# Modulation sums spread over the input tiles, and mLSTM norms set between the output tiles, in an fp32 two-block kernel

## The reference

```python
mod = silu(c) @ w_ada + b_ada                       # 6 x 1024 values: sh1, sc1, gt1, sh2, sc2, gt2
h = rmsnorm(x, g_norm1) * (1 + sc1) + sh1
z = h @ w_in                                        # glu_a, glu_b, q, k, v, o, i, f, g_a, g_b
u = causal_dwconv(glu_a * sigmoid(glu_b))           # 31 taps
y_a = silu(layernorm(u)) @ w_conv_out
q, k = silu(causal_dwconv(q, k))                    # 4 taps
hm = mlstm(q, k, v, i, f)                           # 4 heads of 128: weighted scores, numerator,
                                                    # denominator max(|den|, exp(-m)), division
hm = layernorm_per_head(hm) * m_norm_g * sigmoid(o)
y_b = hm @ w_m_out
x = x + gt1 * ((sigmoid(g_a) * y_a + sigmoid(g_b) * y_b) @ w_out)
...                                                 # then router, experts, and a second block
```

## Time and profile before

| | us |
|---|---|
| median of 3 runs | 2563.48 (2561.7 to 2565.02) |
| the profiled execution | 2564.16 |
| its span, first to last instruction | 2562.4 |
| PE busy in the span | 2313.2 |
| DVE busy in the span | 1182.8 |
| ACT busy in the span | 813.5 |
| mean granted TensorE clock | 0.942 of full speed |

### The profile page before, as it was taken

The page is one execution under the profiler, slowest core; times in us unless marked ns, Lnnn a source line. Parts: engine busy times, 40 slices in busy tenths (PEclk is TensorE's granted clock), DMA queues, the critical chain, the costliest instruction groups (busy, mean ns, idle before and its releaser), DMA issues.

```text
span 2562.4 us, 29704 instructions
## 1 busy us (share of the span) xinstructions
PE 2313.2 (90%) x11748; PEld 1584.8 (62%) x11748; DVE 1182.8 (46%) x1716; ACT 813.5 (32%) x1251; POOL 119.6 (5%) x160
## 2 busy tenths in 40 slices
PE   6899878959999999957989498999999899999997
PEld 3688636623333333324768496888777787888775
DVE  3789345430000000025654743677843573677832
ACT  3222333321111111124455253323324283323322
POOL 0000000021111111100000200000000000000000
PEclk8999978979999999978989689999999999999999
DMA  8622200628999999830111001122222301222221
GB/s 356 226 79 92 92 0 33 277 91 332 375 378 399 386 389 385 359 137 34 66 66 66 1 34 66 66 98 98 99 99 99 132 1 66 81 90 95 95 99 66
DMA packets 36406, 384.56 MB, mean 150 GB/s; under 512 B 10080, under 2 KB 10336, under 8 KB 13408
## 3 DMA queue, kind: packets, MB, share of 16 engines
q1 hardware_dynamic: 27520, 374.91, 37.5%
q0 software_dynamic: 8800, 8.45, 1.0%
HBM read 384.10 MB, written 16.83 MB: 156 GB/s over the span
## 4 chain that ended last, share of the span: by engine, by line
PE 53%; DVE 16%; ACT 5%; issue 3%; DMA 1%; DVEq 1%; POOL 0%; ACTq 0%; SPq 0%; POOLq 0%
PE PS L744 9%; PE PS L570 9%; PE PS L571 9%; PE PS L572 8%; PE PS L783 4%; PE PS L764 4%; DVE ring_r L1946 3%; PE PS L791 2%; DVE A L1694 2%; ACT w_hi_r L1318 2%; PE PS L533 2%; DVE A L2156 1%; DVE sq L2154 1%; DVE A L2157 1%; DVE hid_r L2169 1%
## 5 line engine op out<-in xcount | busy, mean ns | idle before, releaser
L571 PE MATMUL PS<-h_r,w_hi_r 128*128 128x512 f32 x1104 | 432.5, 392 | 0.0
L570 PE MATMUL PS<-h_hi_r,w_hi_r 128*128 128x512 f32 x1056 | 418.0, 396 | 10.8 <-ACT A L1345 7.5
L572 PE MATMUL PS<-h_hi_r,ring_r 128*128 128x512 f32 x1056 | 413.3, 391 | 0.0
L1946 DVE TENSOR_TENSOR ring_r<-ring,w_hi_r 128x1024 fp32r<-128x1024 f32 x196 | 238.6, 1223 | 362.7 <-ACT w_hi_r L1318 362.7
L1318 ACT ACTIVATE w_hi_r<-ring 128x1024 fp32r<-128x1024 f32 x196 | 202.6, 1051 | 329.0 <-PE PS L572 203.9
L570 PEld LDWEIGHTS PS<-h_hi_r,w_hi_r 128*128 128x128 f32 x1056 | 199.7, 189 | 62.3 <-issue 17.2
L571 PEld LDWEIGHTS PS<-h_r,w_hi_r 128*128 128x128 f32 x1104 | 209.2, 190 | 45.0 <-issue 1.9
L572 PEld LDWEIGHTS PS<-h_hi_r,ring_r 128*128 128x128 f32 x1056 | 199.6, 189 | 42.1
L1922 DVE TENSOR_TENSOR A<-A,PS 128x512 f32<-128x512 f32 x16 | 11.0, 687 | 396.4 <-PE PS L744 396.4
L744 PE MATMUL PS<-A 128*64 128x512 f32 x768 | 170.4, 600 | 0.1
L570 PE MATMUL PS<-x_r,top_r 128*128 128x512 f32 x320 | 128.2, 400 | 12.0 <-DVE ring_r L1605 12.0
(11 more groups left out here) (448 smaller groups left out, 3762.6 us busy)
## 6 DMA issues: line engine op xcount, KB each, us to landing
A<-wexp SPq DMA_DIRECT2D x64, 2048.0 KB, 12.3
ring<-wall SPq DMA_DIRECT2D x63, 2048.0 KB, 8.1
ring<-wexp SPq DMA_DIRECT2D x16, 2048.0 KB, 18.1
h<-wexp SPq DMA_DIRECT2D x16, 2048.0 KB, 13.2
A<-wada SPq DMA_DIRECT2D x12, 2048.0 KB, 14.7
x<-xt_in SPq DMA_DIRECT2D x2, 2048.0 KB, 12.1
A<-y_assignments SPq DMA_DIRECT2D x4, 1024.0 KB, 7.9
h_tokens<-A SPq DMA_DIRECT2D x4, 512.0 KB, 2.8
```

The source lines that it names most:

```text
L570: mm(out, w[0], x_[0], start=first, stop=False)
L571: mm(out, w[0], x_[1], start=False, stop=False)
L572: return mm(out, w[1], x_[0], start=False, stop=last_)
L1946: tt(ring_r[:, slot, :, cols], ring[:, slot, :, cols], w_hi_r[:, :, cols].bitcast(F32), ALU.subtract).then_inc(S("w_lo"), 1)
```

## The change

1. SP: unit 0 is issued before quarter 4. Quarters 6 and 7 are now DVE's as well; quarters 8, 9 are issued before unit 3, 10 and 11 before unit 5, each when its buffer is free.
2. PE, prologue: each `ada_cols` follows its own `ada_rows`; rows of quarter 4 come after the gate products. ACT's copy of them moves behind the x_r copies.
3. PE, input tiles: rows only of quarter 5; columns of quarters 4 to 11 one at a time after tiles 0, 1, 8, 9, 16, 17, 20 and 21, in three banks, with four `mod_ev`.
4. The transposes of v come after tile 36, the conv mean and gate columns after tile 37, the conv variance after tile 38; ACT's copies, SiLUs and squares move with them. Heads' convolutions go in the order q0, k0, q1, k1, ...
5. Heads: numerators alternate between banks 6 and 3; DVE weights head h + 1 before it divides head h; the row of exp(-m) comes after the next scores; the conv norm's scaling and SiLUs sit behind head 0's weights.
6. Out tiles: tiles wait for their own bank (`mix_bank`) instead of a whole group; means of the heads stand before tile 2, variances before tile 4; the DVE norm operations are interleaved with the gating.

```diff
-                if a in (4, 5):
-                    sp.wait_ge(S("ada_row"), a - 3)
-                elif a in (6, 7, 8, 9):
-                    sp.wait_ge(S("ada_row"), a - 1)
-                elif a >= 10:
-                    sp.wait_ge(S("ada_used"), a - 9)
+                if 4 <= a < 8:
+                    sp.wait_ge(S("ada_row"), a - 3 if a < 6 else a - 1)
+                elif a >= 8:
+                    sp.wait_ge(S("ada_used"), a - 7)
...
+            load_first(0)
             load_ada(4)
-            load_first(0)
...
-            for a in range(6, 10):
+            for a in range(6, 8):
                 load_ada(a)
             for u in range(2, NU1):
-                if u == 3:
-                    for a in range(10, 12):
+                if u in (3, 5):
+                    for a in range(u + 5, u + 7):
                         load_ada(a)
...
-            ada_rows(0)
-            for a in range(1, 4):
+            for a in range(4):
                 ada_rows(a)
-                ada_cols(a - 1, 1)
-            ada_cols(3, 1)
-            ada_rows(4)
+                ada_cols(a, 1)
...
+            ada_rows(4)
...
-                    if g == 0:
-                        ada_cols(4 + j, 6)
-                        if j < 3:
-                            ada_rows(5 + j)
...
+                    if j < 2 and g in (0, 2, 4, 5):
+                        n = (0, 2, 4, 5).index(g)
+                        ada_cols(4 + 2 * n + j, MOD_BANK[n])
+                    if p == 0:
+                        ada_rows(5)
+                    if p == 36:
+                        v_rows()
+                    if p == 37:
+                        conv_mean()
+                        gate_columns()
+                    if p == 38:
+                        conv_var()
...
             for hd in range(MH):
                 if hd:
-                    pe.wait_ge(S("ml_h"), hd)
-                head_row(hd, 5, gr[7])
+                    pe.wait_ge(S("ml_ad"), hd)
                 for s in range(NT):
                     pe.wait_ge(S("ml_p"), NT * hd + s + 1)
-                    mm(PS[:, 6, s * P:T], A[:, 16 + s, hd * P:(hd + 1) * P], A[:, 52 + s, s * P:T], start=s == 0,
+                    mm(PS[:, num_bank(hd), s * P:T], A[:, 16 + s, hd * P:(hd + 1) * P], A[:, 52 + s, s * P:T], start=s == 0,
                        stop=s == NT - 1)
...
                 if hd + 1 < MH:
                     head_scores(hd + 1)
...
+                head_end(hd)
...
+            pe.wait_ge(S("h_lo"), KD + CT)
+            for q in range(8):
+                if q == 2:
+                    head_means()
+                if q == 4:
+                    head_vars()
+                if q >= 4:
+                    pe.wait_ge(S("ev_dve"), q - 3)
+                out_tile_of(q, lambda k: h_r[:, k, :], lambda k: h_hi_r[:, 2 + k, :])
             pe.wait_ge(S("ml_std"), MH)
...
+            pe.wait_ge(S("h_lo"), 2 * KD)
+            for q in range(8, 16):
+                if q >= 12:
+                    pe.wait_ge(S("ev_dve"), q - 7)
+                out_tile_of(q, lambda k: hid_r[:, 16 + k, :], lambda k: hid_r[:, 8 + k, :])
...
-            for a in range(8, 12):
+            for a in range(6, 8):
                 ada_acc(a)
...
             for i in range(CT):
                 conv_u(i)
-            for m in range(8):
+                if i == 0:
+                    for a in range(8, 12):
+                        ada_acc(a)
+            for m in HEAD_ORDER:
                 w_lo_in(9 + m)
                 conv_qk(m)
...
+            head_rows(0)
+            head_weights(0)
+            conv_normed()
+            for hd in range(MH):
                 if hd + 1 < MH:
                     head_rows(hd + 1)
...
+                    head_weights(hd + 1)
+                head_divided(hd)
...
+            gated(0)
+            out_w_lo(4)
+            gated(1)
...
             for hd in range(MH):
...
+                head_normed(hd)
+                gated(4 + hd)
+                out_w_lo(8 + hd)
             for hd in range(MH):
...
                 dve.wait_ge(S("h_hi"), KD + CT + hd + 1)
                 tt(hid_r[:, 8 + hd, :], A[:, 8 + hd, :], hid_r[:, 16 + hd, :].bitcast(F32), ALU.subtract).then_inc(S("h_lo"), 1)
```

More of the change, by code:

```diff
@@ L598, in _ @@
                     last.then_inc(S("mm"), 1)
-                    if g == 0:
-                        ada_cols(4 + j, 6)
-                        if j < 3:
-                            ada_rows(5 + j)
[L604 to L629, removed]
+                    if j < 2 and g in (0, 2, 4, 5):
[10 more added lines that the diff above has]
+                        conv_var()
+            pe.wait_ge(S("g_rows"), 2)
+            pe.wait_ge(S("em"), 1)
             pe.wait_ge(S("gT_ev"), 1)
-            pe.wait_ge(S("cl_ev"), 1)
-            pe.wait_ge(S("em"), 1)
             def head_row(hd, bank, src):
@@ L655, in _ @@
                     head_scores(hd + 1)
[L657 to L663, removed]
-            pe.wait_ge(S("ml_std"), MH)
[L666 to L695, removed]
@@ L696, in _, with head_means, head_vars @@
-            norm(1, 4 * (G_WOUT % 2))
+                head_end(hd)
+            def head_means():
+                pe.wait_ge(S("ml_h"), MH)
+                for hd in range(MH):
+                    mm(PS[:, 4 + hd, :], ones, A[:, 8 + hd, :], start=True, stop=True).then_inc(S("ml_mu"), 1)
+            def head_vars():
+                for hd in range(MH):
+                    pe.wait_ge(S("ml_sq"), hd + 1)
+                    mm(PS[:, 4 + hd, :], ones, A[:, 12 + hd, :], start=True, stop=True).then_inc(S("ml_var"), 1)
@@ new lines, in out_tile_of @@
+            def out_tile_of(q, u_hi, u_lo):
+                slot, ks, cols = out_piece(q)
+                pe.wait_ge(S("w_lo"), PIECES_IN + q + 1)
+                w_lo = ring_r[:, slot, ks, cols]
+                for k in range(CT):
+                    last = product(PS[:, mix_bank(q), :], (out_hi(q)[:, k, :], w_lo[:, k, :]), (u_hi(k), u_lo(k)), k == 0, k == CT - 1)
+                last.then_inc(S("mm"), 1)
+            pe.wait_ge(S("h_lo"), KD + CT)
[7 more added lines that the diff above has]
+                out_tile_of(q, lambda k: h_r[:, k, :], lambda k: h_hi_r[:, 2 + k, :])
@@ new lines, in _ @@
+            pe.wait_ge(S("ml_std"), MH)
+            pe.wait_ge(S("h_lo"), 2 * KD)
[3 more added lines that the diff above has]
+                out_tile_of(q, lambda k: hid_r[:, 16 + k, :], lambda k: hid_r[:, 8 + k, :])
+            for p in range(KD):
+                pe.wait_ge(S("ev_dve"), p + 9)
+                pe.wait_ge(S("w_lo"), PIECES_IN + 16 + p + 1)
+                for k in range(KD):
+                    if p == 0:
+                        pe.wait_ge(S("h_lo"), 2 * KD + k + 1)
+                    last = product(PS[:, mix_bank(16 + p), :], (in_hi(p)[:, k, :], ring_r[:, unit_slot(f"w_out{p // 4}"), k, (p % 4) * P:(p % 4 + 1) * P]),
+                                   (merged_hi(k), a_r(24 + k)[:, 0, :]), k == 0, k == KD - 1)
+                last.then_inc(S("mm"), 1)
@@ L698, in _ @@
+            norm(1, NORM_BANK[1])
             freed(pe, 15)
@@ L1170, in w_hi_in @@
                     a_(in_hi(p), ring[:, g % 2, :, j * P:(j + 1) * P], ACT.Copy).then_inc(S("w_hi"), 1)
-            for a in range(5):
+            for a in range(4):
                 ada_rows_out(a)
@@ L1248, in _ @@
                 a_(A[:, 12 + hd, :], A[:, 8 + hd, :], ACT.Square).then_inc(S("ml_sq"), 1)
+            for q in range(5, 8):
+                out_w_hi(q)
             for hd in range(MH):
@@ L1610, in step @@
                     w_lo_in(min(pieces[0] + 1, PIECES_IN))
-                    for n, p, bank in ((1, 6, 6), (2, 15, 7)):
-                        if pieces[0] == p:
-                            mod_ev(n, bank)
+                    if pieces[0] in MOD_PIECES:
+                        n = MOD_PIECES.index(pieces[0])
+                        mod_ev(4 + 2 * n, 2, MOD_BANK[n])
             def ada_acc(a):
```

201 lines of the change are left out of this document (132 added, 69 removed).

## The result

The changed kernel takes 2517.72 us in the median of 4 runs (2513.54 to 2523.63), the kernel before 2562.59 (2555.64 to 2565.02): ratio 0.9835, interval 0.9818 to 0.9851. Forecast was 2525.5, in a range of 2513 to 2539. The profiled execution took 2513.93 us and has a span of 2512.2. It is near the lower end of its kernel's runs, and the profiled execution of the kernel before (2564.16) near the upper end of its own, so the two profiles lie 50.2 us apart where the medians lie 44.9 apart.

The account below looks back on a forecast made before the run. TensorE (PE) is busiest, but stages before the router have different limits. Five stages sum to 462.8 instead of 503.5 us (-40.7); with +2.7 for clock falls, 2563.5 - 38 = 2525.5 us, 8 in 10 within 2513 to 2539.

Parts of the forecast that it names:

- bounds 51.0 and 55.7: Prologue: first tile at 52.6 us instead of 54.1; columns cost +1.3 at full clock, +6.3 at the lower, +3.2 taken.
- Tile 14: Input tiles: VectorE waits for quarter 10's transfer, so this tile is 5.8 us late and loses 1.9 of clock.
- No pause at group 3: Input tiles: the clump of 16 column sums at 137.94 us goes away, -6.8 us.
- Rival B: Input tiles: VectorE reaches quarter 10 some 6 us later, so tile 14 is on time; 2517.5 us, chance 0.12.
- the distance from head 0 to head 1: Heads: head 1's numerators follow head 0's at 12.0 us, where the kernel before took 13.5.
- Rival C: Heads: the clock falls in each 1.5 us gap and PE is the bound; +20 us, 2545.5, chance 0.12.
- Rival E: Tile 38 to out tile 7: PE keeps 1.2 GHz; +64 us, 2589, chance 0.04.
- the 5 us that the stage would have had on top: Heads: at the skill page's 2.66 us per table switch, four switches ahead of head 1's weights add an estimated 5 us.
- idle at tile 8: Out tiles: PE waits 5.6 us before tile 8 for VectorE's four hid splits behind tile 7's gating, losing 1.9 of clock.
- 4.8 us of idle before the third tile: w_out: the third tile's low piece stands behind the wait for x, 4.8 us of idle plus 1.9 of slow clock.
- let the first tile start at once: w_out: gatings keep pace, so the first tile no longer starts 2.3 us late with 1.9 of slow clock.
- Five falls at 0.5 more: +2.7: Surcharge on the sum: each fall of the clock was charged 1.9 us, and five may cost 0.5 more, +2.7.

Follow-up runs that it names:

- four profiles: The changed kernel, unaltered, profiled four times: once for the result and three times more; medians 2517.72, 2516.53 and 2522.67 us, and one run of 2523.33 us.
- three other kernels with the same prologue: Changed kernel with x reloaded sooner (2521.63 us), with low pieces handed out sooner (2505.96 us), and with all four repairs (2493.34 us).
- fourth profile: The changed kernel, nothing altered, run once more for its stages alone: one run of 2523.33 us, the only profile from the upper group of runs.
- first profile: The changed kernel as profiled for the result, against the kernel before: profiled execution 2513.93 us, median 2517.72 us, ratio 0.9835.
- the one with x sooner: Changed kernel with the reload of x issued before the second half of w_out instead of behind it: 2521.63 us, 0.9847 of the kernel before.

## Why the prediction came out as it did

The mechanism was right in four stages and partly in w_out; 2525.5 was 7.8 us high, within the range.

**Prologue.** Forecast 52.6, bounds 51.0 and 55.7; the four profiles have 50.7 to 53.5, and three other kernels with the same prologue 55.8 to 56.0. The columns waited 1.45 us (the first) and 0.7 us (the others) for ACT's copy, and the rows ran at either clock, so the two ends of the forecast were right within 0.3 us.

**Input tiles.** 255.5 against 255.7 to 256.0. Tile 14 was forecast 7.7 us late, and by ACT's timeline is 8.3 late (the copy that waits for its end starts at 151.95, that for tile 13 at 138.18, and a tile is 5.44). No pause at group 3. Rival B, the wait that doesn't come, is refuted in all four profiles, though the median of 2517.7 happens to be its time: a total alone would have named the wrong cause.

**Heads.** 46.3 against 43.2 in three profiles and 46.2 in the fourth. The mis-sized term is the distance from head 0 to head 1: 12.0 is near the 12.4 of the fourth profile, where the first numerators run at the lower clock, and it is 9.4 where they don't. The forecast does not split its 12.0, so whether it held a slow clock isn't on record. The others were 10.1 and 10.7, measured 10.0 and 10.6. Rival C needed the fall in every gap: it came in one or two of them, clock 0.96 or 0.89 against the 0.79 of before. Rival E is far off. Table loads took what the trace of before said, as ACT's timeline shows ahead of head 0's weights:

```profile
308.13 1.28 ACT L1185 ACT_TABLE_LOAD   x1
309.43 0.69 ACT L1185 ACTIVATE rstd<-PS,eps 128x512 f32<-128x512 f32 x1
```

The next instruction starts 1.30 us after the load does. The Trainium skill (ScalarE: Activation LUTs, "What ACT_TABLE_LOAD costs") adds a drain, 2.66 us in all; it doesn't show here, nor do the 5 us that the stage would have had on top.

**Out tiles.** 58.1 against 57.7, and 5.15 us of idle at tile 8 where 5.6 was forecast.

**w_out: the step that failed in size.** Forecast 50.3, of it 4.8 us of idle before the third tile and 1.9 of slow clock behind it; measured 47.4, with 1.47 us of idle and no fall (clock 1.00). x landed 12.8 us after its issue instead of 13.9. And the forecast let the first tile start at once, with the gatings keeping pace; it came 0.4 us late and stood 1.2 us more ahead of its last six products, for splits that DVE had still to do behind the gatings. With that, less of the wait for x was left to the third tile. "Five falls at 0.5 more: +2.7" wasn't needed either.

In the first profile these make 9.9 us: prologue 1.3, heads 3.1, w_out 2.9 (forecast less measured), the surcharge 2.7, out tiles 0.4, tiles -0.5; the rest, taken as unchanged, was 2.3 shorter. The fourth profile has five stages of 463.0 us where my sum had 462.8. That is partly luck: w_out was forecast 3.3 too long, out tiles 2.3 and the prologue 0.9 too short. The forecast stands near the upper of this kernel's runs and not in the middle of them: 7 of its 15 timed runs are under 2518 us, 4 of them under 2514.

**Open.** Why the clock falls behind the same idle in one execution and not in another is not settled by these runs. The moved transposes, means and variances were not tried alone, and the small gain in the rest (about 1 us of the 2059) has no cause that I can name.

## What to carry to other kernels

The chain of PE, VectorE and PE with a long division in it was shortened only when the result bank and the order on the second engine changed together; taking back either alone cost all 20 us. When a load is moved to cure a wait, walk the queue to where its buffer comes free: the wait comes back there, and the cure was to put work between the release and the use. And where idles of 1 to 6 us are spread over a kernel, judge a small edit by the stages of its profile and not by the medians of a few runs.

## What the runs showed of the hardware

The clock did not follow the length of the idle before it. In the first profile of the changed kernel products went on at full speed behind idles of 2.91 us (head 0) and 1.47 us (w_out) and at half speed behind 0.96 us (head 2); in the fourth the same 2.91 us was followed by half speed. A stretch at the lower clock cost 1.4 us (seven products) to 3.0 us (heads, fourth profile). The Trainium skill (TensorE: Matmul & The Clock Gate, "Part 1: The HAM clock gate") has the chip judge PE's activity on a rhythm of its own that is not reset by the kernel, so that the same code may turn slow in different places; the four profiles agree with that. The same holds for the prologue, whose instructions are the same in the changed kernel and in the one with x sooner: with all four groups of modulation rows at 1.92 us it took 50.7 us, with three of them at 2.89 to 3.64 us 55.8.
